# Value projection of a cross-attention as eight units of 512-column matmuls, with four output tiles begun before the last two heads, in a two-layer decoder kernel

## The reference

```python
def _memory_cross_attn(h, mem_n, w_q, w_kv, w_o):
    q = (h @ w_q).reshape(bsz, seq, XA_HEADS, XA_HEAD_DIM)      # 4 heads of 256
    k, v = jnp.split(mem_n @ w_kv, 2, axis=-1)                  # mem_n: 256 x 1024
    s = jnp.einsum("bshd,bmhd->bhsm", q, k) * (XA_HEAD_DIM ** -0.5)
    p = jax.nn.softmax(s, axis=-1)
    o = jnp.einsum("bhsm,bmhd->bshd", p, v).reshape(bsz, seq, D_MODEL)
    return o @ w_o
```

## Time and profile before

| | us |
|---|---|
| median of 3 runs | 1319.8 |
| lowest, highest | 1319.52, 1322.51 |
| the profiled execution: its time | 1319.97 |
| its span | 1318.2 |
| TensorE busy in it | 1291.9 (98%) |
| VectorE busy | 1000.5 (76%) |
| ScalarE busy | 762.0 (58%) |
| GpSimd busy | 237.7 (18%) |

### The profile page before, as it was taken

The page is one execution under the profiler, slowest core; times in us unless marked ns, Lnnn a source line. Parts: engine busy times, 40 slices in busy tenths (PEclk is TensorE's granted clock), DMA queues, the critical chain, the costliest instruction groups (busy, mean ns, idle before and its releaser), DMA issues.

```text
span 1318.2 us, 24123 instructions
## 1 busy us (share of the span) xinstructions
PE 1291.9 (98%) x8348; PEld 1178.8 (89%) x8348; DVE 1000.5 (76%) x1541; ACT 762.0 (58%) x1375; POOL 237.7 (18%) x324
## 2 busy tenths in 40 slices
PE   7999999999999999999999999999999999999997
PEld 6888889989997888888888888999989998888886
DVE  5788777678668888777888668998967767888854
ACT  6555544356556655555556447778855655655642
POOL 2233110112001111111111101024451201111111
PEclk9999999999999999999999999999989999999999
DMA  6656645545444656645556645444445544555660
GB/s 211 214 191 193 218 163 173 180 159 176 145 130 158 195 188 201 220 154 172 192 185 218 199 153 178 158 155 130 129 128 193 176 145 130 183 185 188 224 202 36
DMA packets 60551, 228.32 MB, mean 173 GB/s; under 512 B 6848, under 2 KB 7360, under 8 KB 60352
## 3 DMA queue, kind: packets, MB, share of 16 engines
q1 hardware_dynamic: 60048, 226.60, 52.9%
q10 hardware_dynamic: 432, 0.79, 0.2%
HBM read 226.31 MB, written 1.05 MB: 172 GB/s over the span
## 4 chain that ended last, share of the span: by engine, by line
PE 83%; DVE 8%; ACT 4%; issue 2%; POOL 1%; DMA 0%; DVEq 0%; ACTq 0%; SPq 0%; POOLq 0%
PE bank L1263 83%; DVE w_lo L741 3%; ACT w_hi L374 2%; DVE acc L744 2%; DVE acc L741 1%; DVE x L741 1%; ACT sq L407 1%; ACT corr L374 1%; DVE t L741 0%; DVE h L744 0%; DMA x<-x_t 0%; PE bank L1412 0%; DVE m L741 0%; ACT xd L374 0%; DVE a L744 0%
## 5 line engine op out<-in xcount | busy, mean ns | idle before, releaser
L741 DVE TENSOR_TENSOR w_lo<-raw,w_hi 128x1024 fp32r<-128x1024 f32 (+2 forms) x403 | 521.4, 1297 | 38.8 <-ACT w_hi L374 37.0
L1263 PE MATMUL bank<-h,w_hi 128*128 128x512 f32 (+1 forms) x2056 | 480.3, 362 | 11.9 <-DVE h L744 6.8
L374 ACT ACTIVATE w_hi<-raw 128x1024 fp32r<-128x1024 f32 (+2 forms) x403 | 442.6, 1099 | 52.1 <-PE bank L1263 51.4
L1263 PEld LDWEIGHTS bank<-h,w_hi 128*128 128x128 f32 x2056 | 357.4, 192 | 60.8 <-DVE h L744 8.6
L1263 PE MATMUL bank<-a,w_hi 128*128 128x512 f32 (+1 forms) x1664 | 365.0, 344 | 1.0 <-POOL a L1185 0.7
L1263 PEld LDWEIGHTS bank<-a,w_hi 128*128 128x128 f32 x1664 | 283.3, 191 | 32.2 <-POOL a L1185 1.1
L1263 PE MATMUL bank<-h,w_lo 128*128 128x256 f32 x1736 | 291.1, 283 | 0.0
L1263 PEld LDWEIGHTS bank<-h,w_lo 128*128 128x128 f32 x1736 | 257.6, 192 | 14.6
L374 ACT ACTIVATE corr<-bank 128x256 f32<-128x256 f32 x233 | 88.6, 381 | 266.7 <-PE bank L1263 266.7
L1263 PE MATMUL bank<-a,w_lo 128*128 128x256 f32 x1280 | 230.8, 283 | 0.0
L1263 PEld LDWEIGHTS bank<-a,w_lo 128*128 128x128 f32 x1280 | 193.6, 191 | 7.2
(11 more groups left out here) (184 smaller groups left out, 1135.8 us busy)
## 6 DMA issues: line engine op xcount, KB each, us to landing
raw<-w_gu SPq DMA_DIRECT2D x174, 512.0 KB, 3.5
raw<-w_down SPq DMA_DIRECT2D x64, 704.0 KB, 4.1
raw<-w_xbc SPq DMA_DIRECT2D x32, 512.0 KB, 3.6
raw<-w_conv_in SPq DMA_DIRECT2D x24, 512.0 KB, 3.6
raw<-w_q SPq DMA_DIRECT2D x16, 512.0 KB, 4.0
raw<-w_k SPq DMA_DIRECT2D x16, 512.0 KB, 3.6
raw<-w_v SPq DMA_DIRECT2D x16, 512.0 KB, 3.5
raw<-w_o SPq DMA_DIRECT2D x16, 512.0 KB, 3.7
```

The costliest lines, as they stand in the source:

```text
L374: return nc.scalar.activation(out, in_, ACT.Copy, scale=scale)
L741: return nc.vector.tensor_tensor(out, a, b, op)
L1263: return nc.tensor.matmul(out, lhs, rhs, start=start, stop=stop, skip_group_check=check)
```

## The change

The v weights are laid out as 512-column blocks (`_wide` in place of `_natural`), and the v steps call `wide_unit`, which the z projection of the SSD mixer already used. Four units now make 512 columns (two heads) in two banks, so V is evicted twice a layer in pieces of 128 x 512 (`v_part`) in place of four times in pieces of 128 x 256. The turns, the products with V, `pt_part` and `o_part` are moved to other steps. Before the last two heads are there, TensorE runs four output tiles over four blocks each; then the four tiles over blocks 4 and 5, and then over 6 and 7. The four slots therefore hold the units of tiles 0 to 3 at once; the split of tile 3's unit is made ahead of `project_out`, and that function's first split is left out for the output projection.

On ScalarE:

```diff
             def project_out(phase, per_tile):
                 for k in range(KT):
                     for u in range(per_tile):
-                        split(n0 + per_tile * k + u + AHEAD)
+                        if k or phase[0] != "o":
+                            split(n0 + per_tile * k + u + AHEAD)
...
+                    elif s == 17:
+                        pt_part(layer, 0)
+                    elif s == 19:
+                        v_part(layer, 0)
+                    elif s == 21:
+                        pt_part(layer, 1)
+                        o_part(layer, 0)
+                    elif s == 23:
+                        pt_part(layer, 2)
+                        o_part(layer, 1)
+                        v_part(layer, 1)
+                pt_part(layer, 3)
+                o_part(layer, 2)
                 o_part(layer, 3)
                 project_out(f"o{layer}", 1)
+            def v_part(layer, c):
+                act.wait_ge(unit_done, first[f"v{layer}"] + 4 * c + 4)
+                for mt in range(2):
+                    copy(v_hi[:, mt, c * 512:c * 512 + 512], bank[2 * c + mt][:, :], rms_mem_n[:, mt:mt + 1]).then_inc(kv_hi, 1)
```

On VectorE, whose `pt_part`, `o_part` and `v_part` stand in the same steps as ScalarE's:

```diff
             def project_out(phase, per_tile, banks, scale):
-                    if k < KT - 1 or OUT_NORM[phase] > 7:
+                    if (k or phase[0] != "o") and (k < KT - 1 or OUT_NORM[phase] > 7):
                         split(n0 + per_tile * (k + 1) - 1 + AHEAD)
```

On TensorE:

```diff
             def attention(layer):
-                        natural_unit(n0 + s, outs, 4 * u, mn_hi, mn_lo, u == 0, u == 1)
+                        wide_unit(n0 + s, outs, 2 * u, mn_hi, mn_lo, u == 0, u == 3)
...
-                early = 2 * HEADS - 2
-                output_tile(layer, 0, 0, early)
-                wait_v(layer, 3)
-                values(layer, 3)
-                output_tile(layer, 1, 0, early)
-                for t in range(KT):
-                    output_tile(layer, t, early if t < 2 else 0, KT)
+                early = HEADS
+                output_tile(layer, 0, 0, early)
+                turn(layer, 3)
+                output_tile(layer, 1, 0, early)
+                wait_v(layer, 1)
+                values(layer, 2)
+                output_tile(layer, 2, 0, early)
+                output_tile(layer, 3, 0, early)
+                values(layer, 3)
+                for t in range(4):
+                    output_tile(layer, t, early, early + 2)
+                for t in range(KT):
+                    output_tile(layer, t, early + 2 if t < 4 else 0, KT)
```

More of the change, by code:

```diff
@@ L85, in plan @@
         n += units
-        tiles = units // 2 if name[:4] == "down" or name in ("z", "ssd_out") else units if units > 1 else 0
+        tiles = units // 2 if name[:4] == "down" or name[0] == "v" or name in ("z", "ssd_out") else units if units > 1 else 0
         banks = 2 if name[:4] == "down" else 4
@@ L252, in trunk @@
         FFN_A = {0: 0, 1: FT + KT + KT, 2: 2 * FT + 2 * KT, 3: 3 * FT + 3 * KT}
+        KV_PARTS = KT + 4
         CONV_A, Q_A = FT, {0: FT + KT, 1: 3 * FT + 2 * KT}
@@ L502, in attention @@
                 n0 = first[f"q{layer}"]
-                for s in range(24):
+                for s in range(25):
                     if s != 1:
                         split(n0 + s + AHEAD)
+                    if s == 24:
+                        break
                     if s == 0:
@@ L517, in attention @@
                                                      bias=neg_mx[:, tt:tt + 1], accum_out=tot[:, tt:tt + 1]).then_inc(exp_ready, 1)
-                        if s == 19 + 2 * h:
-                            o_part(layer, h)
                     if s < KT:
@@ L943, in attention @@
                         if k >= 2:
-                            dve.wait_ge(kv_hi, 16 * layer + k - 1)
+                            dve.wait_ge(kv_hi, KV_PARTS * layer + k - 1)
                         tt(gate[s % 2][:, :], bank[s % 4][:, 0:N_MEM], rms_mem[:, :]).then_inc(evac[s % 4], 1)
                         split(n0 + s + AHEAD)
-                        dve.wait_ge(kv_hi, 16 * layer + k + 1)
+                        dve.wait_ge(kv_hi, KV_PARTS * layer + k + 1)
                         rest_of(k_lo[:, k, :], gate[s % 2][:, :], k_hi[:, k, :]).then_inc(k_ready, 1)
-                    elif s % 2 == 0:
-                        split(n0 + s + AHEAD)
-                    else:
[L952 to L960, removed]
+                    else:
+                        if s == 17:
+                            pt_part(layer, 0)
+                        if s == 19:
+                            v_part(layer, 0)
+                        if s == 21:
+                            pt_part(layer, 1)
+                            o_part(layer, 0)
+                        if s == 23:
+                            pt_part(layer, 2)
+                            o_part(layer, 1)
+                            v_part(layer, 1)
                         split(n0 + s + AHEAD)
@@ L964, in attention, with v_part @@
                             softmax_norm(layer, h)
+                split(n0 + 24 + AHEAD)
+                pt_part(layer, 3)
+                o_part(layer, 2)
                 o_part(layer, 3)
                 project_out(f"o{layer}", 1, 4, None)
+            def v_part(layer, c):
+                for mt in range(2):
+                    dve.wait_ge(kv_hi, KV_PARTS * layer + KT + 2 * c + mt + 1)
+                    b = 2 * c + mt
+                    cols = slice(c * 512, c * 512 + 512)
+                    stt(v_lo[:, mt, cols], bank[b][:, :], rms_mem_n[:, mt:mt + 1], v_hi[:, mt, cols].bitcast(F32),
+                        op1=ALU.subtract).then_inc(evac[b], 1)
             def mem_rest(layer, k):
@@ L1424, in values @@
                 ins.then_inc(o_done, 1)
[L1426 to L1438, removed]
             def attention(layer):
@@ L1460, in attention @@
                             scores(h)
[L1461 to L1465, removed]
-                early = 2 * HEADS - 2
-                output_tile(layer, 0, 0, early)
-                wait_v(layer, 3)
+                    if s == 17:
+                        turn(layer, 0)
+                    if s == 19:
+                        turn(layer, 1)
+                    if s == 20:
+                        wait_v(layer, 0)
+                        values(layer, 0)
+                    if s == 22:
+                        values(layer, 1)
+                        turn(layer, 2)
+                early = HEADS
+                output_tile(layer, 0, 0, early)
+                turn(layer, 3)
[4 more added lines that the diff above has]
+                output_tile(layer, 3, 0, early)
                 values(layer, 3)
-                output_tile(layer, 1, 0, early)
+                for t in range(4):
+                    output_tile(layer, t, early, early + 2)
                 for t in range(KT):
-                    output_tile(layer, t, early if t < 2 else 0, KT)
+                    output_tile(layer, t, early + 2 if t < 4 else 0, KT)
             def output_tile(layer, t, k0, k1):
@@ L1484, in output_tile, with wait_v @@
                     ins.then_inc(unit_done, 1)
-            def wait_v(layer, h):
+            def wait_v(layer, c):
                 for mt in range(2):
-                    vb, use = bank_use(f"v{layer}", 2 * h + mt)
+                    vb, use = bank_use(f"v{layer}", 2 * c + mt)
                     pe.wait_ge(evac[vb], use + 1)
@@ L1731 @@
         "w_k": np.stack([_units(w[:, :D_MODEL]) for w in t["xa_w_kv"]]),
-        "w_v": np.stack([_natural(w[:, D_MODEL:]) for w in t["xa_w_kv"]]),
+        "w_v": np.stack([_wide(w[:, D_MODEL:]) for w in t["xa_w_kv"]]),
         "w_o": np.stack([_units(w) for w in t["xa_w_o"]]),
```

5 lines of the change are left out of this document (1 added, 4 removed).

## The result

| | us |
|---|---|
| before, median of 20 runs | 1319.84 (1316.85 to 1323.27) |
| changed, median of 20 runs | 1321.72 (1320.91 to 1324.46) |
| ratio, 95% interval | 1.0019 (1.0011 to 1.0027) |
| changed, span of the profiled execution | 1319.4 |

The change made the kernel slower by 0.19%, some 2.5 us by the ratio and 1.9 by the medians, where 6.5 us had been forecast. The direction is right, the size is not, and 1321.72 lies under the range. The 20 times of the changed kernel stand in two groups, 12 from 1320.91 to 1322.03 and 8 from 1323.38 to 1324.46, so its mean, 1322.40, is above its median; the kernel before has a mean of 1319.99.

The account below looks back on a forecast made before the run. TensorE, busy 98% of the span, bounds nearly everything, but a ScalarE-VectorE loop sets the output projection's end. A layer: -0.96 + 4.20 + 0 + 0 = +3.24 us; two +6.5, from 1319.8 to 1326.3 us, range 1322.2 to 1329.8.

Parts of the forecast that it names:

- V with 512 columns: V steps of each layer: 96 wide matmuls replace 192 of 256 columns, 0.96 us less a layer.
- The 0.24 us that I had worked out from the Trainium skill: V steps: gain a layer from 96 fewer matmuls at about 2.5 ns each; time would be near 1327.7.
- 4.20 us of tiles ahead of tile 0's end: Output projection: six blocks each of two more tiles now precede tile 0's end, 4.20 us a layer.
- No new wait up to tile 0's end: V evictions and rests ready before TensorE wants them: cost 0, cover 0.5 us at its thinnest.
- The loop of 21.46 us: ScalarE and VectorE handing over tiles, from tile 0's end to tile 6's h: 2.99 us a turn, unchanged.
- the gap of 3.5 us: New TensorE wait ahead of output tile 4, costing nothing of its own because the wait for h follows.
- The work after the wait is TensorE's own again and shifts whole: After the wait for h: each layer's +3.24 us carries through fully, +6.5 us over two layers.
- a rival at 0.12: Slow clock behind new gap narrows gap ahead of h, sparing 1.7 us (1324.6); with faster loop 1322.4; chance 0.12.
- 1329.7 as a rival: Slow matmuls after every long gap, four times: at most 1329.7 us; the slower outcome near 1329.5 had chance 0.17.
- faster: Output projection: loop behind tile 0 runs quicker than 2.99 us a turn, down to 1313.5 us; chance 0.07.

Follow-up runs that it names:

- e3: Changed kernel with each 512-column matmul of the value projection cut into two of 256 columns: 1327.88 us.
- e8: Changed kernel with every gap filled, tile 0 finished before tiles 2 and 3 get blocks 4 and 5 and before tile 1's last two: 1316.60 us.
- e4: Changed kernel with two output tiles begun early in place of four: 1321.52 us, ratio 1.0010.
- e5: Kernel before with unread matmuls in every TensorE idle stretch over 1 us after the start: 1313.03 us, ratio 0.9951.
- e6: Changed kernel with every gap filled by unread matmuls, 14 of them ahead of output tile 4: 1318.99 us, ratio 0.9993.
- e9: Kernel before with only the wait at the end of the SSD mixer filled (10 unread matmuls): 1317.07 us, ratio 0.9980.
- e10: Changed kernel with only the wait at the end of the SSD mixer filled: 1321.20 us.
- e12: Kernel before, unaltered, run once more for a second profile: single time 1320.70 us.
- e15: Kernel before with 5 unread 512-column matmuls (1.15 us) ahead of the third SwiGLU: 1319.56 us, ratio 1.0011.
- e16: Kernel before with 10 unread 512-column matmuls (2.3 us) ahead of the third SwiGLU: 1321.54 us, ratio 1.0022.
- e11: Changed kernel, unaltered, run once more for a second profile: single time 1319.21 us.
- e13: Changed kernel with 5 unread 512-column matmuls (1.15 us) ahead of the third SwiGLU: 1325.66 us, ratio 1.0049.
- e14: Changed kernel with 10 unread 512-column matmuls (2.3 us) ahead of the third SwiGLU: 1323.55 us, ratio 1.0040.
- e1: Kernel before with 8 unread matmuls in each wait for h behind the output projection, and 10 put behind the SSD wait by mistake: 1320.92 us, ratio 1.0005.
- e2: Changed kernel with the waits for h and the gap ahead of output tile 4 filled, 10 matmuls misplaced behind the SSD wait: 1324.38 us, ratio 1.0042.

## Why the prediction was wrong

*V with 512 columns*: forecast -0.96 us a layer by the rows of z; e3 puts the width at 1.14. Right, slightly undersized. The 0.24 us that I had worked out from the Trainium skill ("TensorE: Matmul & The Clock Gate", "Wait — 56ns, not 53.3ns?") does not agree with e3's 1.14; the measurement decides.

*4.20 us of tiles ahead of tile 0's end*: right. Together with V 3.05 measured against 3.24. e8 shows that it is the place that counts: 1.4 us moved behind tile 0's end, less a short wait, gave 1.12 a layer.

*No new wait up to tile 0's end*: right; TensorE was busy for all of it. e4 shows how near it was: with two tiles taken away, 0.45 and 0.76 us of wait appear.

*The loop of 21.46 us is fixed, and the gap of 3.5 us costs nothing of its own*: right, 21.46 and 3.51.

*The step that failed is the sum's last one*: "The work after the wait is TensorE's own again and shifts whole", with no term for the clock, which was left to a rival at 0.12. The work did shift whole where nothing fell (649.48 us between the layers in e5, 649.49 in e6). But the kernel before does not run without falls, and the change spares it some. By the medians, filling the gaps takes 6.8 us off the kernel before (1319.84 to 1313.03) and 2.7 off the changed one (1321.72 to 1318.99). The 4.1 us between are what the forecast lacked; by the means they are 3.4. In these, the SSD wait is 2.3 by the medians (2.8 in e9 less 0.5 in e10) and 1.5 by the means (2.8 less 1.2).

The rest, 1.8 or 1.9 us, fits the waits for `h`, though no run filled them alone. In the kernel before, a fall stands behind layer 0's in all five profiles that leave it unfilled (before, e9, e12, e15, e16; some 1.5 us in e9, 650.95 us between the layers in place of 649.49) and behind layer 1's in two of them (e9, e15). In the changed kernel it stands behind neither, in any of the six profiles that leave them unfilled (the first, e3, e10, e11, e13, e14). In all but one of these twelve places a fall ahead of output tile 4 delays TensorE and leaves a gap of at most 1.6 us in place of 2.2, which is the mechanism of my rival, worked out there as 1.7 us. The one left over, layer 1 of e10, says that this is not all: no fall stands behind its gap of 3.51 us, the full 2.17 us of the wait for `h` are there, and no fall follows these either. I had treated layer 1's 1.00 as an even chance, from one profile. The SSD fall I missed, since I read the clock only where the change is made.

The rule of the Trainium skill, "TensorE: Matmul & The Clock Gate", "What's actually happening", that the slow clock is the default and activity releases it, had given 1329.7 as a rival. In the first profile the fall behind the new gap came in both layers, as it says; its price was covered by the later wait, and the wait for `h` that was left had no fall behind it. In e10's layer 1 tile 4's first matmuls run at full speed straight behind the same gap, 2.07 us for eight in place of 3.75:

```profile
1107.97 2.07 PE L1285 MATMUL bank<-a,w_hi 128*128 128x512 f32 x8 [3.51 <-DVE w_lo L753]
```

*The rivals*: "faster" is refuted by the loop's 2.98 us. The one with the clock named a right mechanism, and that its 1322.4 is so near 1321.72 is in part luck: the clock's share in it was 1.7 us (1324.6), the other 2.2 were to come from a faster loop, which did not come, and the SSD fall, which it did not have, stands in that place.

## What to carry to other kernels

Where two engines hand tiles to each other more slowly than TensorE makes them, the start of their loop sets the end: whatever is placed ahead of the first tile's end is paid in full, and a tile begun early is only worth it if it covers a wait that is there. A gap of 2 to 3 us on TensorE can cost, beside its own length, a fall of the clock (some 1.5 us behind a wait for `h`, 2.8 behind the SSD wait in the kernel before), and whether the fall comes can change with microseconds moved elsewhere, so a change of a few us should be judged with the gaps filled in both versions: here that turned 1.9 us with overlapping runs into 6.0 us with none. Filling the gaps with matmuls that nobody reads is also the fastest version found: the kernel before with five fills, 1313.03 us, 0.49% (0.35 to 0.63) below the kernel before and 8.7 us below the changed one.

## What the runs showed of the hardware that I had not expected

The same wait of 2.57 us, with the same work around it, is followed by slow matmuls or not according to when it comes: of the twelve profiles that leave the SSD wait open, seven have the fall (before, e1, e3, e4, e12, e13, e16) and five don't (changed, e2, e11, e14, e15). In the kernel before the fall was regular enough to cost 2.8 us in the median of 12 runs.

What fixes this, no run here controlled. The kept traces hold one pointer, which is an argument from them and not a test. In each of the 17 profiles with more than one fall, the beginnings of all its falls are whole multiples of one and the same interval apart, whatever the kernel did between them. They follow a beat that the program doesn't set, and it stands differently against the program in two executions of one kernel. In the changed kernel's first profile a point of this beat comes 1.24 us into the SSD wait, and no fall follows; in the kernel before's none lies inside the wait, and one follows. So it may be the wait's place against this beat, rather than its distance from the earlier falls, that goes with the fall.
